# A product that adds a causal mask to the running maxima of an mLSTM scan, on fp32r operands instead of fp32 ones

## The chip, the cores and the metric

One Trainium2 chip, one core of it. The time is that of one execution on the device in microseconds (us), and lower is better. TensorE is called PE in the profile (PEld is its weight load), VectorE DVE, ScalarE ACT, GpSimd POOL, and SyncE SP.

## The reference

Two layers of a hybrid block over 256 context and 1024 latent tokens of width 1024. Each layer has a token mixer of four head groups and a feed-forward part: dense in the first layer, a mixture of eight experts in the second. The change lies in the mixer, where two recurrences run over the tokens in both directions. One is gated linear attention (GLA), the other the mLSTM, cut here to what the change touches:

```python
def mlstm_scan(q, k, v, ig, lf, state, with_output):
    ...
    cum = jnp.cumsum(lf, axis=3)
    ...
    mask = jnp.tril(jnp.ones((L, L), dtype=bool))
    d_log = jnp.where(mask, cum[..., :, None] - cum[..., None, :] + ig[..., None, :], -jnp.inf)
    inter_log = cum + m_prev[..., None]
    m_row = jnp.maximum(inter_log, jnp.max(d_log, axis=-1))
    s = jnp.exp(d_log - m_row[..., None]) * jnp.einsum('bhnld,bhnsd->bhnls', q, k)
    ...
```

The weight of source token s for target token l is an exponential, and it is zero where s lies behind l in the direction of the scan. The kernel gets that zero by adding 1e30 to the running maximum at the masked places before it takes the exponential of (value of s minus that maximum).

## The kernel before

The program is a row of phases with a barrier of all engines after each one, so nothing of a phase overlaps the next. In each of the two layers they are: a norm, the input projection, a Fourier mix, a spatial gate, the decays (`phase_decays`), the scan (`phase_scan`), the output gates, the output projection, and then the feed-forward part with its own norm. `phase_scan` (L809) is the one that the change touches. It runs once in each layer.

**The work of a scan.** The 1280 tokens stand in 10 tiles of 128. A unit is one tile in one direction, and a scan has 20 of them (`for u in range(U)`), the forward (`d = 0`) and the backward direction in turn. Each engine runs the same loop over the units with its own list of instructions, written out by hand. Semaphores tie the lists together. There is no scheduler.

**One unit on TensorE, in order.** All of it is fp32, and the profile records every fp32 product as two MATMUL and two LDWEIGHTS, the transposes as one each:

- L854, L856: transposes of a decayed key and of two key tiles.
- L861: identity times a 128x512 mask (`negF` or `negB`, 1e30 where masked and 0 elsewhere, four copies side by side, one for each head), written to the PSUM bank `MB` with `start=True`. For u of 1 and more it waits for `a_ex` of the unit before, that is for ScalarE's last read of that bank.
- L863: four products of depth 8, one for each head, that add the running maxima `mx`, broadcast over the 128 source rows, into the same bank. The last one raises `pe_mb`.
- L870: the mLSTM scores. It waits for `g_q`, GpSimd's masked copies of q, and for `v_w` of the unit before.
- L877: the GLA scores. It waits for `v_st` of the unit before, the new states of VectorE (in the first unit for `v_init`, VectorE's zeroing).
- L882, L884: products with the states `Sp` and `Sm`.
- L887: the GLA output. It waits for `v_sg`, VectorE's masked copy of the GLA scores (L950).
- L892: the mLSTM output. It waits for `v_w`, VectorE's product of weights and scores (L954).
- L897, L900: the updates of the states. The last one raises `pe_u`.

**The other engines.** ScalarE copies the transposed key out of PSUM (L911), then takes four exponentials of the bank `MB` into `ex` (L914). GpSimd makes the masked copies of q (L925, L927), two units ahead of TensorE's use of the buffers at most. VectorE has the longest list: `kw` (L947), L950, L954, the read of the GLA output (L958 or L960), then from L963 on the mLSTM output with its denominator (L963 to L977; where the tile has been written by the other direction, L974 and L975 take the place of L977), and then the updates of the states from L981 to L990. L990 writes `Sp` and raises `v_st`. Many of these steps wait for the one before them by a semaphore (`Chain`).

Of the kernel before, what the change touches and what calls it, by code (L numbers as in the profile page):

```python
# [15 lines left out]
F32R = mybir.dt.float32r  # L16
# [6 lines left out]
P = 128  # L23
# [9 lines left out]
NH, HD = 4, 64  # L33
# [775 lines left out]
def phase_scan(nc, io, S, l, FM, TM, M):  # L809

    U = 2 * NT
    with Phase(nc, f"scan{l}") as ph:
# [15 lines left out]
        g_q = ph.sem("masked_q_ready")  # L828
        qg = ph.sb("qg", [P, 2, NH, P])
        qm = ph.sb("qm", [P, 2, NH, P])  # L830
        v_init, v_kw, v_sg, v_w, v_og, v_om, v_st, ch = (ph.sem(n) for n in (
            "states_zero", "kw_ready", "gla_weights_ready", "mlstm_weights_ready", "gla_out_read", "mlstm_out_read", "states_ready", "dve_step"))
        ps, c = S["ps"], S["c"]
        mx, tg, dcol, qd, kd, em, vx, og, om = (M[k] for k in ("mx", "tg", "dcol", "qd", "kd", "em", "vx", "og", "om"))
        TR, SG, OG, KT, MB, SM, OI, OC = range(8)
# [3 lines left out]
        def unit(u):  # L839
            d = u % 2  # L840
            n = order(d, u // 2)
            return d, n, slice(n * P, (n + 1) * P)

        with nc.Block() as block:

            @block.tensor
            def _(pe):
                for u in range(U):
                    d, n, t = unit(u)

                    if u >= 1:
                        pe.wait_ge(a_kdt, u)
                        pe.wait_ge(v_kw, u)
                    nc.tensor.transpose(ps[:, KT, 0:P], kd[:, d, t], c("ident"))  # L854
                    for j in range(2):
                        x = nc.tensor.transpose(ps[:, TR, (j + 1) * P:(j + 2) * P], FM[:, mk[j], t], c("ident"))  # L856
                    x.then_inc(pe_tr, 1)

                    if u >= 1:
                        pe.wait_ge(a_ex, u)  # L860
                    nc.tensor.matmul(ps[:, MB, :], c("ident"), c("negF" if d == 0 else "negB"), start=True, stop=False, skip_group_check=True)  # L861
                    for h in range(NH):
                        x = nc.tensor.matmul(ps[:, MB, h * P:(h + 1) * P], sel8[0:8, 4 * d + h, :], mx[:, d, t],  # L863
                                             start=False, stop=(h == NH - 1), skip_group_check=True)
                    x.then_inc(pe_mb, 1)
                    if u >= 1:
                        pe.wait_ge(v_w, u)
                    pe.wait_ge(g_q, u + 1)
                    for j in range(2):
                        x = nc.tensor.matmul(ps[:, SM, j * 256:(j + 1) * 256], FM[:, mk[j], t],  # L870
                                             qm[:, d, 2 * j:2 * j + 2, :].rearrange("p a b -> p (a b)"), start=True, stop=True)
                    x.then_inc(pe_sm, 1)
                    if u >= 1:
                        pe.wait_ge(v_st, u)
                    else:
                        pe.wait_ge(v_init, 1)
                    nc.tensor.matmul(ps[:, SG, :], kd[:, d, t], qg[:, d, :, :].rearrange("p a b -> p (a b)"),  # L877
                                     start=True, stop=True).then_inc(pe_sg, 1)
                    if u >= 1:
                        pe.wait_ge(v_og, u)  # L880
                        pe.wait_ge(v_om, u)
                    nc.tensor.matmul(ps[:, OG, 0:256], qd[:, d, t], Sp[:, d, :], start=True, stop=False, skip_group_check=True)  # L882
                    for j in range(2):
                        nc.tensor.matmul(ps[:, OC, j * 130:(j + 1) * 130], FM[:, mq[j], t], Sm[:, d, j, :], start=True, stop=True)  # L884
                    pe.wait_ge(v_sg, u + 1)
                    for h in range(NH):
                        x = nc.tensor.matmul(ps[:, OG, h * HD:(h + 1) * HD], sg[:, d, h, :], TM[:, n, h * HD:(h + 1) * HD],  # L887
                                             start=False, stop=(h == NH - 1), skip_group_check=True)
                    x.then_inc(pe_og, 1)
                    pe.wait_ge(v_w, u + 1)  # L890
                    for h in range(NH):
                        x = nc.tensor.matmul(ps[:, OI, h * 65:(h + 1) * 65], ex[:, d, h, :], vx[:, n, h, :], start=True, stop=True)  # L892
                    x.then_inc(pe_om, 1)

                    pe.wait_ge(a_kdt, u + 1)
                    pe.wait_ge(v_og, u + 1)
                    nc.tensor.matmul(ps[:, OG, 256:512], kdt[:, d, :], TM[:, n, 0:256], start=True, stop=True)  # L897
                    pe.wait_ge(v_kw, u + 1)
                    for j in range(2):
                        x = nc.tensor.matmul(ps[:, SG, j * 130:(j + 1) * 130], kw[:, d, 2 * j:2 * j + 2, :].rearrange("p a b -> p (a b)"),  # L900
                                             vx[:, n, 2 * j:2 * j + 2, :].rearrange("p a b -> p (a b)"), start=True, stop=True)
                    x.then_inc(pe_u, 1)

            @block.scalar
            def _(act):
                for u in range(U):
                    d, n, t = unit(u)
                    if u >= 2:
                        act.wait_ge(pe_u, u - 1)
                    act.wait_ge(pe_tr, u + 1)  # L910
                    nc.scalar.copy(kdt[:, d, :], ps[:, KT, 0:P]).then_inc(a_kdt, 1)  # L911
                    act.wait_ge(pe_mb, u + 1)
                    for h in range(NH):
                        x = nc.scalar.activation(ex[:, d, h, :], ps[:, MB, h * P:(h + 1) * P], ACT.Exp,  # L914
                                                 bias=tg[:, n, d, 0, 4 * d + h:4 * d + h + 1], scale=-1.0)
                    x.then_inc(a_ex, 1)
# [1068 lines left out]
def build(nc, io):  # L1985
    S = {name: nc.dram_tensor(name, shape, F32, kind="Internal").ap() for name, shape in
         (("xT_d", (P, KD, T)), ("mixT_d", (P, KD, T)), ("xs_d", ((NUNIT + 1) * UNIT, D)), ("ys_d", (NUNIT * UNIT, D)), ("g2_d", (D,)), ("a_d", (P, DFF // P, T)))}
    with ExitStack() as top:
# [11 lines left out]
        for l in range(2):  # L2000
            ctx_out = l == 0
            groups = GROUPS if ctx_out else GROUPS[1:]
            with ExitStack() as lay:
                FM = sb(lay, f"FM{l}", [P, 9, T])
                TM = sb(lay, f"TM{l}", [P, NT, 1536])
                with ExitStack() as st:
                    hT = sb(st, f"hT{l}", [P, KD, T])

                    xT = TM[:, 0:7, :].rearrange("p a b -> p (a b)")[:, 0:KD * T].rearrange("p (k t) -> p k t", t=T)
                    phase_norm(nc, S, f"nm{l}", io["xT"] if l == 0 else S["xT_d"], xT, hT, l, 0, GROUPS)  # L2010
                    phase_project(nc, io, S, l, hT, FM, TM, ctx_out)
                phase_fourier(nc, io, S, l, FM, ctx_out)
                phase_sgu(nc, io, S, l, TM, ctx_out)
                M = {}
                M["qd"] = sb(lay, f"qd{l}", [P, 2, T])
                M["kd"] = sb(lay, f"kd{l}", [P, 2, T])
                M["em"] = sb(lay, f"em{l}", [P, 2, 3, NT])
                M["mx"] = sb(lay, f"mx{l}", [8, 2, T])
                M["ig"] = sb(lay, f"ig{l}", [8, T])
                M["tg"] = sb(lay, f"tg{l}", [P, NT, 2, 4, 8])  # L2020
                M["dcol"] = sb(lay, f"dcol{l}", [P, 4, NT])
                M["vx"] = sb(lay, f"vx{l}", [P, NT, NH, 65])
                phase_decays(nc, io, S, l, FM, TM, M)

                for name, ch in (("og", 0), ("om", 6)):
                    M[name] = FM[:, ch:ch + 2, :].rearrange("p a b -> p (a b)").rearrange("p (n c) -> p n c", c=256)
                phase_scan(nc, io, S, l, FM, TM, M)
                phase_mix_out(nc, io, S, l, TM, M, ctx_out)
# [67 lines left out]
```

## Time and profile before

| what | us |
|---|---|
| median of 3 runs | 6039.61 |
| lowest and highest of them | 6039.34 and 6043.22 |
| the profiled execution, its own time | 6042.35 |
| its span in the profile | 6040.4 |

The busy times of the whole span are 5266.8 us for TensorE, 2766.7 us for VectorE, 2003.3 us for ScalarE and 163.9 us for GpSimd. The two scans fill about 753 to 931 us and 2793 to 2971 us of it. The clock column (PEclk) gives the TensorE clock that was granted: 1.00 is 2.4 GHz, 0.50 is 1.2 GHz. The "idle before" of a row names what ended the idle time of that engine. The end of a matmul record is modelled, so records of products that follow each other overlap, and the time that a product takes from its engine is read from start to start.

### The profile page before, as it was taken

How to read it: one execution, taken by the hardware profiler on the slowest of the kernel's cores; microseconds unless marked ns; L12 is line 12 of the kernel's file. 1: busy time of each engine (PE TensorE's matmuls, PEld its weight loads, DVE VectorE, ACT ScalarE, POOL GpSimd, SP SyncE). 2: the span in 40 equal slices, each digit the busy share in tenths (PEclk: the TensorE clock that was granted, in tenths of full speed). 3: DMA queues.
4: the chain of work that ended last, by engine and by line, in shares of the span. 5: the costliest groups of instructions: out<-in, count | busy, mean ns of one | idle time of the engine just before them, and what ended most of it. 6: DMA issues, size and time to landing. Idle time of an engine off the chain costs nothing. (4 is left out here: it accounts for less than half of the span.)

```text
span 6040.4 us, 61280 instructions
## 1 busy us (share of the span) xinstructions
PE 5266.8 (87%) x22972; PEld 3985.7 (66%) x22973; DVE 2766.7 (46%) x2881; ACT 2003.3 (33%) x1995; POOL 163.9 (3%) x239
## 2 busy tenths in 40 slices
PE   6899395699997969975675999999999999999994
PEld 3444174488886755433555888888888888888883
DVE  0220474311113332116623844599659654448466
ACT  1100111211112230002112634477547544447453
POOL 0000020000000000001101000000000000000001
PEclk7899697799998989987885999999999999999996
DMA  9111003221115441010036955599759755558576
GB/s 382 28 43 52 18 1 133 80 65 56 57 46 169 135 148 31 22 65 1 23 139 262 346 186 197 206 381 380 256 207 382 293 183 204 196 182 340 200 274 226
DMA packets 262623, 996.66 MB, mean 165 GB/s; under 512 B 40000, under 2 KB 112384, under 8 KB 175744
## 3 DMA queue, kind: packets, MB, share of 16 engines
q1 hardware_dynamic: 243200, 926.43, 41.7%
q0 software_dynamic: 13040, 49.29, 2.2%
q10 hardware_dynamic: 6288, 19.66, 0.8%
q8 instruction: 61, 1.00, 0.1%
q14 instruction: 34, 0.28, 0.0%
HBM read 911.68 MB, written 83.63 MB: 165 GB/s over the span
## 5 line engine op out<-in xcount | busy, mean ns | idle before, releaser
L1697 PE MATMUL ps<-moe_gate_up_hi,moe_xh 128*128 128x512 f32 x2464 | 963.0, 391 | 9.3 <-DVE moe_gate_up_lo L1849 9.3
L1697 PE MATMUL ps<-moe_gate_up_hi,moe_xl 128*128 128x512 f32 x2464 | 960.7, 390 | 0.0
L1849 DVE TENSOR_TENSOR moe_gate_up_lo<-moe_wst,moe_gate_up_hi 128x2048 fp32r<-128x2048 f32 x424 | 952.2, 2284 | 17.7 <-ACT moe_gate_up_hi L1780 17.7
L1697 PE MATMUL ps<-moe_gate_up_lo,moe_xh 128*128 128x512 f32 x2464 | 959.6, 389 | 0.0
L1780 ACT CAST moe_gate_up_hi<-moe_wst 128x2048 fp32r<-128x2048 f32 x424 | 791.1, 1924 | 0.1
L1862 DVE TENSOR_TENSOR moe_down_lo<-moe_wst,moe_down_hi 128x2048 fp32r<-128x2048 f32 x210 | 480.1, 2289 | 159.1 <-ACT moe_down_hi L1794 158.6
L1697 PEld LDWEIGHTS ps<-moe_gate_up_hi,moe_xh 128*128 128x128 f32 x2464 | 463.2, 188 | 106.8 <-DVE moe_gate_up_lo L1849 11.6
L1697 PEld LDWEIGHTS ps<-moe_gate_up_hi,moe_xl 128*128 128x128 f32 x2464 | 463.2, 188 | 96.9
L1697 PEld LDWEIGHTS ps<-moe_gate_up_lo,moe_xh 128*128 128x128 f32 x2464 | 463.3, 188 | 95.5
L1868 DVE TENSOR_TENSOR moe_a<-moe_sil,ps 128x512 f32<-128x512 f32 x210 | 143.4, 683 | 739.2 <-ACT moe_sil L1800 739.2
L1800 ACT ACTIVATE moe_sil<-ps 128x512 f32<-128x512 f32 x210 | 125.9, 600 | 982.5 <-PE ps L1697 982.4
L1794 ACT CAST moe_down_hi<-moe_wst 128x2048 fp32r<-128x2048 f32 x210 | 404.2, 1925 | 72.6 <-PE ps L1717 72.6
L1256 PE MATMUL ps<-hh,up_wh 128*128 128x512 f32 (+1 forms) x1056 | 376.8, 357 | 51.2 <-DVE up_wl L1300 39.4
L1717 PE MATMUL ps<-moe_down_hi,moe_ah 128*128 128x512 f32 x1232 | 399.2, 405 | 9.7 <-DVE moe_al L1873 9.7
L403 PE MATMUL ps<-proj_w,hT 128*128 128x512 f32 x928 | 398.6, 592 | 0.0
L1717 PE MATMUL ps<-moe_down_lo,moe_ah 128*128 128x512 f32 x1232 | 383.0, 392 | 0.0
L1717 PE MATMUL ps<-moe_down_hi,moe_al 128*128 128x512 f32 x1232 | 380.4, 390 | 0.0
L1256 PE MATMUL ps<-hl,up_wh 128*128 128x512 f32 (+1 forms) x1056 | 374.4, 355 | 0.0
L1256 PE MATMUL ps<-hh,up_wl 128*128 128x512 f32 (+1 forms) x1056 | 374.2, 354 | 0.0
L400 PE MATMUL ps<-hT,proj_w 128*128 128x512 f32 (+1 forms) x832 | 307.9, 534 | 48.2 <-DMA proj_w<-in_w_in 48.2
L403 PEld LDWEIGHTS ps<-proj_w,hT 128*128 128x128 f32 x928 | 176.3, 190 | 221.9 <-issue 221.9
L400 PEld LDWEIGHTS ps<-hT,proj_w 128*128 128x128 f32 x832 | 161.3, 194 | 194.8 <-issue 136.8
(330 smaller groups left out, 6499.5 us busy)
## 6 DMA issues: line engine op xcount, KB each, us to landing
moe_wst<-in_moe_packed SPq DMA_DIRECT2D x634, 1024.0 KB, 6.7
ada_w<-in_ada_packed SPq DMA_DIRECT2D x24, 2048.0 KB, 26.4
down_wst<-in_ffn_w_down SPq DMA_DIRECT2D x66, 512.0 KB, 3.6
proj_w<-in_w_in SPq DMA_DIRECT2D x8, 2048.0 KB, 7.8
four_dft<-in_dft_seq SPq DMA_DIRECT2D x16, 1024.0 KB, 4.9
xs_d<-route_zero SPq DMA_DIRECT2D x1, 16384.0 KB, 50.8
moe_rows<-xs_d POOLq DMA_DIRECT2D x16, 1024.0 KB, 5.3
ys_d<-moe_y POOLq DMA_DIRECT2D x15, 1024.0 KB, 4.5
```

What stands on the lines that cost most here:

```text
L400: mm = nc.tensor.matmul(ps[:, u % NB, :n], wring[:, i % 2, k, j * P:(j + 1) * P], hT[:, k, a:a + n], start=(k == 0), stop=(k == KD - 1))
L403: mm = nc.tensor.matmul(ps[:, u % NB, :], hT[:, k, a * P:(a + 1) * P], wring[:, i % 2, k, :], start=(k == 0), stop=(k == KD - 1))
L1256: x = nc.tensor.matmul(ps[:, 2 * g + kind, :n], w[:, s, kind, k, :], h[:, k, t0:t0 + n], start=(k == 0 and j == 0), stop=(k == KD - 1 and ...
L1697: x = nc.tensor.matmul(ps[:, 2 * (q % 2) + i, :], xx[:, k, t], w[:, q % 2, k, :], start=(k == 0 and j == 0), stop=(k == KD - 1 and j == 2))
L1717: x = nc.tensor.matmul(ps[:, Y0 + 2 * i + half, :], aa[:, q % 2, i, c, :], w[:, q % 2, c, half * 512:(half + 1) * 512], start=(q == 0 and ...
L1780: nc.scalar.copy(guh[:, q % 2, 4 * j:4 * j + 4, :], wst[:, slot(n), :].rearrange("p (k n) -> p k n", k=4)).then_inc(hi, 1)
L1794: nc.scalar.copy(dnh[:, q % 2, :, :], wst[:, slot(n), :].rearrange("p (k n) -> p k n", k=2)).then_inc(hi, 1)
L1800: nc.scalar.activation(sil[:, :, :], ps[:, 2 * (q % 2):2 * (q % 2) + 2, 0:W], ACT.Silu).then_inc(silu, 1)
L1849: nc.vector.tensor_tensor(gul[:, q % 2, k, :], wst[:, slot(n), :].rearrange("p (k n) -> p k n", k=4), guh[:, q % 2, k, :].bitcast(F32), AL ...
L1862: nc.vector.tensor_tensor(dnl[:, q % 2, :, :], wst[:, slot(n), :].rearrange("p (k n) -> p k n", k=2), dnh[:, q % 2, :, :].bitcast(F32), AL ...
L1868: nc.vector.tensor_tensor(a[:, q % 2, :, :, :].rearrange("p i c f -> p i (c f)"), sil[:, :, :], ps[:, 2 * (q % 2):2 * (q % 2) + 2, W:2 * W ...
```

## The change

At the start of each scan ScalarE rounds three 128x128 tiles to fp32r, the format that TensorE takes in one pass: the identity and one copy of each mask. The mask product then reads these. Its moving operand is the one 128x128 mask, read four times with a step of zero between heads, and its output is the same 128x512 bank. In the first unit of a scan it waits for the rounding. All other products stay as they are.

```diff
@@ phase_scan
         qm = ph.sb("qm", [P, 2, NH, P])
+        unit_r = ph.sb("unit_r", [P, P], F32R)
+        neg_r = ph.sb("neg_r", [P, 2, P], F32R)
+        a_mask = ph.sem("masks_rounded")
...
                     if u >= 1:
                         pe.wait_ge(a_ex, u)
-                    nc.tensor.matmul(ps[:, MB, :], c("ident"), c("negF" if d == 0 else "negB"), start=True, stop=False, skip_group_check=True)
+                    if u == 0:
+                        pe.wait_ge(a_mask, 1)
+                    nc.tensor.matmul(ps[:, MB, :].rearrange("p (h t) -> p h t", t=P), unit_r[:, :],
+                                     neg_r[:, d, :].unsqueeze(1).to_broadcast([P, NH, P]), start=True, stop=False, skip_group_check=True)
...
             @block.scalar
             def _(act):
+                nc.scalar.copy(unit_r[:, :], c("ident"))
+                nc.scalar.copy(neg_r[:, 0, :], c("negF")[:, 0:P])
+                nc.scalar.copy(neg_r[:, 1, :], c("negB")[:, 0:P]).then_inc(a_mask, 1)
                 for u in range(U):
```

ScalarE's list around the start of the first scan, before and then after (dec is the phase of the decays, scan that of the scan):

```order
63 L723 ACTIVATE dec_dec<-dec_dec 8x20
64 L655 UNCONDITIONAL_BRANCH
65 L904 UNCONDITIONAL_BRANCH
66 L911 COPY scan_kdt<-ps 128x128
67 L914 ACTIVATE scan_ex<-ps,tg 128x128 x4
```

```order
63 L723 ACTIVATE dec_dec<-dec_dec 8x20
64 L655 UNCONDITIONAL_BRANCH
65 L910 UNCONDITIONAL_BRANCH
66 L912 CAST scan_unit_r<-cst 128x128
67 L913 CAST scan_neg_r<-cst 128x128
68 L914 CAST scan_neg_r<-cst 128x128
69 L920 COPY scan_kdt<-ps 128x128
70 L923 ACTIVATE scan_ex<-ps,tg 128x128 x4
```

Three casts stand ahead of ScalarE's first copy. No other instruction came in. On TensorE the first unit, with its waits, reads so before and after:

```order
269 L854 MATMUL ps<-cst,kd 128x128
270 L856 MATMUL ps<-cst,FM 128x128 x2
271 L861 MATMUL ps<-cst 128x512
272 L863 MATMUL ps<-mx,cst 128x128 x4
273 L870 MATMUL ps<-scan_qm,FM 128x256 [waits scan0_masked_q_ready]
```

```order
269 L857 MATMUL ps<-cst,kd 128x128
270 L859 MATMUL ps<-cst,FM 128x128 x2
271 L866 MATMUL ps<-scan_neg_r,scan_unit_r 128x512 [waits scan0_masks_rounded]
272 L869 MATMUL ps<-mx,cst 128x128 x4
273 L876 MATMUL ps<-scan_qm,FM 128x256 [waits scan0_masked_q_ready]
```

The mask product keeps its place in the order, changes its operands, and in the first unit has a wait that it did not have. In the later units its wait is the same as before. The lists of VectorE and GpSimd are unchanged but for line numbers.

## Rows read from the trace of the kernel before

**Rows 1.** The page, costs by engine: busy us, share of the span, instructions.
```profile
PE 5266.8 (87%) x22972; PEld 3985.7 (66%) x22973; DVE 2766.7 (46%) x2881; ACT 2003.3 (33%) x1995; POOL 163.9 (3%) x239
```

**Rows 2.** Groups by line and shape, 753 to 930 us (first scan): busy, mean ns.
```profile
L861 PE MATMUL ps<-cst 128*128 128x512 f32 x40 | 21.4, 617 | 0.0
```

**Rows 3.** Waits, 762 to 925 us: who for whom, us, times, longest.
```profile
PEld ps L877 <- DVE scan_Sp L990: 13.6, 19, 1.0
```

**Rows 4.** Timeline of one unit of the first scan: start, us, engine, line.
```profile
764.17 0.43 DVE L963 TENSOR_TENSOR scan_tmp<-ps,tg 128x260 f32<-128x260 f32 x1 [0.47 <-PE ps L892]
...
765.23 1.02 PE L861 MATMUL ps<-cst 128*128 128x512 f32 x2
...
766.19 1.15 PE L863 MATMUL ps<-mx,cst 8*128 8x128 f32 x8
...
767.27 1.13 PE L870 MATMUL ps<-scan_qm,FM 128*128 128x256 f32 x4
...
768.10 0.35 DVE L990 TENSOR_SCALAR scan_Sp<-scan_Sg,em 128x256 f32<-128x256 f32 x1
...
768.49 0.30 PEld L877 LDWEIGHTS ps<-scan_qg,kd 128*128 128x128 f32 x2 [0.50 <-DVE scan_Sp L990]
...
769.66 0.73 DVE L950 COPY_PREDICATED scan_sg<-cst,ps 128x512 f32<-128x512 int32 x1 [0.76 <-PE ps L877]
...
770.45 1.10 PE L887 MATMUL ps<-TM,scan_sg 128*128 128x64 f32 x8
...
772.49 0.43 DVE L963 TENSOR_TENSOR scan_tmp<-ps,tg 128x260 f32<-128x260 f32 x1 [0.47 <-PE ps L892]
```

**Rows 5.** The same, weight load of a unit whose tile was written before.
```profile
785.58 0.30 PEld L877 LDWEIGHTS ps<-scan_qg,kd 128*128 128x128 f32 x2 [0.96 <-DVE scan_Sp L990]
```

**Rows 6.** Timeline of the output projection, TensorE, fp32r products, low and full clock.
```profile
1018.65 0.63 PE L1104 MATMUL ps<-op_mix,op_w_parts 128*128 128x512 f32 x1
...
1019.93 0.63 PE L1104 MATMUL ps<-op_mix,op_w_parts 128*128 128x512 f32 x1
...
1022.28 0.39 PE L1104 MATMUL ps<-op_mix,op_w_parts 128*128 128x512 f32 x1
...
1022.96 0.39 PE L1104 MATMUL ps<-op_mix,op_w_parts 128*128 128x512 f32 x1
```

**Rows 7.** Timeline of the first unit of the first scan.
```profile
753.03 0.18 PEld L854 LDWEIGHTS ps<-cst,kd 128*128 128x128 f32 x1 [1.92 <-issue]
...
753.52 0.55 PEld L861 LDWEIGHTS ps<-cst 128*128 128x128 f32 x2
...
754.14 1.17 POOL L927 TENSOR_TENSOR scan_qm<-FM,cst 128x256 f32<-128x256 f32 x2
...
755.36 0.49 DVE L937 MEMSET scan_Sm<- 128x520 f32 x1
755.57 1.78 PEld L863 LDWEIGHTS ps<-mx,cst 8*128 8x128 f32 x8 [1.50 <-issue]
...
759.44 1.87 PE L877 MATMUL ps<-scan_qg,kd 128*128 128x512 f32 x2
...
762.14 1.10 PE L887 MATMUL ps<-TM,scan_sg 128*128 128x64 f32 x8
```

**Rows 8.** Groups by line and shape, ScalarE: busy us, mean ns.
```profile
L911 ACT COPY scan_kdt<-ps 128x128 f32<-128x128 f32 x40 | 10.6, 266 | 227.3 <-PE ps L856 227.3
L1385 ACT CAST down_ah<-down_ast 128x256 fp32r<-128x256 f32 x22 | 8.8, 400 | 0.0
```

**Rows 9.** Windows: length, busy us (instructions) of PE, PEld, DVE, ACT, POOL, granted clock, DMA share, GB/s.
```profile
757.40:761.80 4.40, 4.40 (x12) 2.79 (x11) 0.45 (x1) 1.14 (x4) 0.39 (x2) 0.58 0.00 0
804.00:925.00 121.00, 116.45 (x671) 87.54 (x670) 90.55 (x233) 19.73 (x70) 28.33 (x39) 1.00 0.00 1
929.00:931.00 2.00, 0.00 (x0) 0.00 (x0) 1.89 (x6) 0.00 (x0) 0.00 (x0) 1.00 0.00 0
1868.00:1892.00 24.00, 19.60 (x156) 18.70 (x156) 10.92 (x14) 9.05 (x15) 0.00 (x0) 1.00 0.58 184
```

## The prediction

> **What bounds the kernel now.** I first read the busy times of the page. They make TensorE look like the bound, at 87% of the span [rows 1]. That share is mostly the projections and the experts, and it says nothing of the scan, so I then read the scan alone. Its window at full clock has TensorE busy for 116.45 of 121 us [rows 9]. A reader would stop here and call every TensorE instruction in it expensive. But a record's end is modelled and records overlap, so "busy" hides small waits. The view that decides is the list of waits, and then the timeline of one unit.
>
> The list of waits has the weight load of L877 waiting 19 times for VectorE's L990, 13.6 us in all, 0.72 us each [rows 3]. That is once for every unit but the first. The timeline shows what this means [rows 4]. In one unit VectorE starts L963 at 764.17 and ends L990 at 768.10 + 0.35 = 768.45. The weight load of L877 starts at 768.49, 0.04 us later. TensorE has its own work meanwhile: L861 from 765.23, L863 from 766.19, L870 from 767.27 to 768.40. So VectorE's piece ends last and releases L877. Then come L877, L950 at 769.66, L887 at 770.45, L892, and L963 again at 772.49. One turn, from L963 to L963, takes 772.49 - 764.17 = 8.32 us, and L861, L863 and L870 are not on it: they lie in TensorE's side branch between the updates of one unit and L877 of the next. In a unit whose tile was written before, VectorE has one more instruction, and the weight load waits 0.96 us instead of 0.50 us [rows 5].
>
> The first unit of each scan is different. No state is pending there, the clock is at its low level, 1.2 GHz, and TensorE works through its list without a real wait until L877 at 759.44, while VectorE's zeroing ended at 755.36 + 0.49 = 755.85 [rows 7]. There L861 is on the path. The clock reaches 2.4 GHz late in the window from 757.40 to 761.80, whose mean is 0.58 [rows 9]. (0.58 - 0.50) x 2 x 4.40 = 0.7 us of it were at the full level, so it rose at about 761.1.
>
> **The warm units (19 of 20 in each scan, 38 in all).** The mask product has 40 records in the first scan, two a unit, of 617 ns on average [rows 2]. They overlap, so the price is read from start to start: it holds TensorE from 765.23 to 766.19, 0.96 us [rows 4]. The nearest price for the new one is the fp32r product of the same shape in the output projection. Three of them pass between two rows of one operand pair, 0.68 us at full clock (1022.28 to 1022.96), or 0.23 us each [rows 6]. So each unit takes 0.96 - 0.23 = 0.73 us off TensorE's branch. The zero step in the moving operand has no row here. I take it at the price of an ordinary operand. At worst it costs as much as before, and since it sits in the branch that is off the path the sum is the same.
>
> Off the path means: L863 and L870 start 0.73 us earlier, L877 still waits for L990, and its weight load now waits about 0.50 + 0.73 = 1.2 us. ScalarE's exponentials (L914) move up by 0.73 us. Nobody waited for them, since VectorE reads `ex` in L954, after L950, which waits for L877. GpSimd is released by L877, which does not move. The warm units therefore give 0 us. The two ends for them: a gain of at most 38 x 0.05 = 1.9 us, if L870's end at 768.40 had some hold on the start of L877 at 768.49, and a loss of nothing from the work itself. I take 0, since L877 follows L990 by the same 0.04 us here.
>
> **The first unit (twice).** Before: the first weight load of L861 starts at 753.52 and that of L863 at 755.57, 2.05 us [rows 7]. After: L861 has to wait for three casts. No row shows a 128x128 cast to fp32r. The 128x256 one takes 400 ns and the 128x128 copy out of PSUM 266 ns [rows 8]. These two are my bounds, and I take 0.29 us, near the copy because the width is the same. The casts start with the phase, at about 753.1 (TensorE's first weight load is at 753.03 [rows 7]), and end at 753.1 + 3 x 0.29 = 754.0. The weights then take 0.27 us (0.55 us for two loads of L861 [rows 7]), and the product itself, at low clock, 1.28 us for three, so 0.43 us [rows 6]. L863 can load at 754.0 + 0.27 + 0.43 = 754.7 instead of 755.57, a gain of 0.9 us, which would be 0.6 us with casts of 0.40 us. ScalarE's own first copy, L911, waits for the transposes until about 754.0 anyway and is not held up. L870 then stands at about 756.6, after GpSimd's copies of that unit (754.14 + 1.17 = 755.31) and after the zeroing (755.85) [rows 7], so the gain reaches L877.
>
> Part of it is given back, because the clock rises by the clock on the wall and not with my work. If it still rises at 761.1, L877 starts 0.9 us earlier, at 758.5, and so does L882, and both run at 1.2 GHz to the end, as does some of L884. L884 and what follows then do at the low level about 0.9 us of work that took 0.45 us at the high one. L887, at 762.14 before [rows 7], comes 0.5 us earlier. The second scan has the same order and the same start, so it gives 0.5 us too.
>
> **Sum.** 38 x 0 - 2 x 0.5 = -1.0 us. Against the profiled execution that is 6042.35 - 1.0 = 6041.4, and against the median, which lies 2.7 us lower, 6039.6 - 1.0 = 6038.6. The phases end in barriers, so what the scans gain passes to the end. The memory of the two new tiles is the scan's own and moves nothing else.
>
> **Rival A, slower: the clock drops inside the scan.** The change lets TensorE stand idle for 1.2 or 1.7 us in every unit. If that brings the clock to 1.2 GHz in the scan, L877 to L900 take twice as long, and these are on the path. A warm unit has about 8.3 - 0.5 - 0.73 = 7.1 us of TensorE work, and cold it takes 14.2 us, which TensorE then bounds: 14.2 - 8.3 = 5.9 us more for each cold unit. Three cold units of 38 make the kernel slower by more than can be told from nothing, and half of them cost 19 x 5.9 = 112 us, 6151 us. Against it: the clock stayed at its full level from 1868 to 1892 us, with TensorE busy for only 19.60 of 24 us, 82% [rows 9]. The changed scan has about 7.1 of 8.3, or 86%. After the last product of the scan TensorE was idle through the whole window from 929 to 931, and the clock was still 1.00 [rows 9]. The gaps that I expect are shorter than that. The Trainium skill, page TensorE: Matmul & The Clock Gate, section "A second HAM failure mode: psum-queue depth-cycling", says that short idles between groups of matmuls, frequent enough, make the clock swing between its levels. By that rule this rival is what happens. The trace does not agree so far, since such idles of 0.5 to 1 us once a unit left the clock at 1.00 for 121 us. I give it 4%.
>
> **Rival B, faster: TensorE's list is the bound after all.** If the waits of 0.5 us in front of L877 are a lead of the weight load over a product that could not have started sooner, each warm unit gets shorter by up to 0.73 us: 38 x 0.73 + 1 = 29 us, 6011 us. For it: L870's end at 768.40 and L877's start at 768.50 nearly touch. Against it: VectorE would have to end its piece earlier too, and L963 to L990 are a closed piece that depends on L892 and L900, not on L861. I give it 3%. The Trainium skill, page TensorE: Matmul & The Clock Gate, section "Back-to-back issue gap", has about 131 ns for a product of 512 columns in a stream of loads and products. The trace says 230 ns [rows 6], so the measurement decides. By the page this rival would gain 0.83 us a unit, 32 us.
>
> **Rival C: the product does not get shorter**, because the repeated operand or the accumulation of fp32 products on top of it costs a full four passes. Nothing in the trace speaks for it, and the total would be 6039.6 plus up to 0.5 us for the wait on the casts in each scan, 6040.6. I give it 3%.
>
> **How the numbers follow.** A measurement of this kernel can tell 0.2%, about 12 us, from no change. My case has 88%, rival A 4%, B 3%, C 3%, and 2% are for a change of the runs that has nothing to do with it. My case and C lie within 12 us. Predicted time 6038.6 us. For the range: the gain can be 1.9 us + 2 x 0.9 = 3.7 us, and the runs of before spread by 3.9 us, which gives 6039.6 - 3.7 - 3.9 = 6032. Upward: no gain, one rise of the clock that comes later in one scan, so that the outputs and updates of the first unit (L887 to L900, about 2.7 us) run at the low level and cost as much again, and the same spread, 6039.6 + 2.7 + 3.9 = 6046. Chances: faster 0.03, same 0.92, slower 0.05.
>
> **What would show it.** Right: one MATMUL of the mask line per unit, 40 in all, of 0.39 us. The weight load of L877's successor waits 1.2 us for VectorE in the shorter units and 1.7 us in the others. A turn of 8.3 or 8.8 us as before. L877 of the first unit at 0.9 us less behind the start of the phase, the next one at 0.5 us less. Clock 1.00 from the second unit on. Wrong: a clock under 1.00 in the middle of a scan (A), a turn under 8.0 us (B), or two records of the mask line per unit (C).

## The result: 0.28% slower

| kernel | median us | lowest to highest | runs |
|---|---|---|---|
| before | 6043.22 | 6039.34 to 6045.48 | 7 |
| changed | 6059.68 | 6054.85 to 6064.69 | 7 |

The ratio is 1.0028, with a 95% interval from 1.0017 to 1.0040, about 17 us. The forecast was 6038.6 us with a range up to 6046, and no difference that can be told. It was wrong, and the time came out on the other side. The profiled execution of the changed kernel took 6060.06 us, its span is 6058.4 us.

In the changed kernel L866 is the mask product, L869 the running maxima, L876 the mLSTM scores, L883 the GLA scores, L888 and L890 the products with the states, L893 and L898 the outputs, L959 VectorE's masked copy, L972 its first step on the mLSTM output, and L999 its write of `Sp`. The page's row of the engines answers to [rows 1]:

```profile
PE 5262.2 (87%) x22932; PEld 3999.0 (66%) x22933; DVE 2767.2 (46%) x2881; ACT 2003.6 (33%) x2001; POOL 163.6 (3%) x239
```

TensorE has 40 records fewer, one for each of the 40 units. Its busy time fell by only 4.6 us, though the records of the mask product fill 9.9 us of each scan instead of 21.4, which is 23 us less in all. Something else got longer. TensorE's weight loads got 13.3 us longer, and no other engine changed by more than 1 us. The windows of the two scans, with the columns of [rows 9], say what it was:

```profile
804.00:925.00 121.00, 109.28 (x610) 86.94 (x610) 84.18 (x219) 18.96 (x68) 28.35 (x39) 0.92 0.00 1
...
2804.00:2966.00 162.00, 144.87 (x815) 114.14 (x816) 112.07 (x287) 25.99 (x93) 43.58 (x60) 0.92 0.00 1
```

The window of the first scan had clock 1.00 and 671 TensorE instructions before [rows 9]. Now it has clock 0.92 and 610, and the records that the mask product no longer has, one a turn, are only some 14 of the 61 that are missing. The waits from 755 to 942 us, in the form of [rows 3], show the idle time that the change makes:

```profile
PEld ps L883 <- DVE scan_Sp L999: 25.5, 19, 1.6
...
PE ps L883 <- DVE scan_Sp L999: 17.9, 19, 1.2
```

The weight load of the GLA scores waited 13.6 us in 19 units before and waits 25.5 us now. The timeline of the first turns, in the form of [rows 4], shows both at work:

```profile
766.74 0.47 PE L866 MATMUL ps<-scan_neg_r,scan_unit_r 128*128 128x512 f32 x1
...
767.14 1.15 PE L869 MATMUL ps<-mx,cst 8*128 8x128 f32 x8
...
768.22 1.13 PE L876 MATMUL ps<-scan_qm,FM 128*128 128x256 f32 x4
...
769.68 0.35 DVE L999 TENSOR_SCALAR scan_Sp<-scan_Sg,em 128x256 f32<-128x256 f32 x1
...
770.08 1.89 PE L883 MATMUL ps<-scan_qg,kd 128*128 128x512 f32 x2 [0.73 <-DVE scan_Sp L999]
...
771.76 1.06 PE L888 MATMUL ps<-scan_Sp,qd 128*128 128x256 f32 x2
...
772.61 1.07 PE L890 MATMUL ps<-scan_Sm,FM 128*128 128x130 f32 x4
...
773.48 1.13 PE L893 MATMUL ps<-TM,scan_sg 128*128 128x64 f32 x8
...
779.86 1.13 PE L883 MATMUL ps<-scan_qg,kd 128*128 128x512 f32 x2 [0.73 <-DVE scan_Sp L999]
```

The branch before L883 runs as forecast. L876 ends at 769.35 and L883 waits 0.73 us for VectorE. But L883 then takes 1.89 us where it took 1.12 us in a warm turn before, and L888 takes 1.06 us where it took 0.59 us. The granted clock of three windows around it:

```profile
770.00:771.00 1.00, 0.92 (x2) 0.41 (x3) 0.45 (x2) 0.00 (x0) 0.00 (x0) 0.66 0.00 0
772.00:773.20 1.20, 1.20 (x5) 1.02 (x5) 1.20 (x2) 0.00 (x0) 1.08 (x2) 0.50 0.00 0
773.20:774.40 1.20, 1.20 (x11) 1.20 (x10) 0.10 (x1) 0.00 (x0) 1.09 (x2) 0.78 0.00 0
```

Just after the wait the clock falls from 2.4 to 1.2 GHz, and some 3.4 us later it is back. From L883 to L883 this turn takes 779.86 - 770.08 = 9.78 us. A turn of that kind takes 8.32 us [rows 4], so one fall costs 1.46 us. In windows of 1 us from the second unit to the last product there are 9 falls in the first scan and 6 in the second, 15 in all. Before there was none. From the first weight load to the end of the last L999 the scans took 177.9 and 178.4 us before and 190.4 and 186.6 us now, 20.6 us more. Fifteen falls are 21.9 us, and the first units gave 1.4 us back (below). That is 20.5 us, so nothing in the scans is left over to explain. The spans of the two profiled executions differ by 18.0 us, so the other phases, which the change does not touch, took 2.6 us less.

Theory: in each turn TensorE stands idle 0.6 us longer, and these idle times let the clock fall on TensorE's part of the path. Rivals: the fp32r format, or the kind of work, brings the falls, and not the idle time.

### The profile page after: what moved, and what is told of

The parts are those of the page before. It is cut to its first block and busy times, and to the rows that moved or that the text cites. A ratio compares the mean times of both kernels' runs of the same rounds, so it can differ in the third digit from the quotient of the medians.

```text
span 6058.4 us, 61208 instructions
## 1 busy us (share of the span) xinstructions
PE 5262.2 (87%) x22932; PEld 3999.0 (66%) x22933; DVE 2767.2 (46%) x2881; ACT 2003.6 (33%) x2001; POOL 163.6 (3%) x239
```

## Experiments

All times are medians beside the kernel before on the same chip, whose median was 6041.61 to 6042.75 us on the chips of the experiments. Falls were counted in the one profiled execution of each kernel, in windows of 1 us, from the second unit to the last product of each scan. "Idle" is the wait of TensorE's products in front of the GLA scores, in shorter and in longer turns, at full clock.

| kernel | idle, us | falls | median us | ratio to before, 95% interval |
|---|---|---|---|---|
| before | about 0.1 / 0.55 | 0 | | 1 |
| changed | 0.72 / 1.19 | 15 | 6059.68 | 1.0028 (1.0017 to 1.0040) |
| product twice | 0.49 / 0.95 | 12 | 6058.59 | 1.0029 (1.0017 to 1.0040) |
| product three times | 0.26 / 0.72 | 13 | 6056.52 | 1.0022 (1.0012 to 1.0032) |
| product four times | 0.02 / 0.49 | 0 | 6042.08 | 1.0000 (0.9991 to 1.0010) |
| product five times | 0 / 0.26 | 0 | 6042.18 | 1.0001 (0.9991 to 1.0011) |
| fp32r forward only | 0.72 / 1.18, every second turn | 1 | 6042.92 | 1.0001 (0.9991 to 1.0011) |
| fp32r in three of four units | 0.72 / 1.19, three of four | 10 | 6052.53 | 1.0018 (1.0008 to 1.0027) |
| fp32, a small VectorE instruction | 0.29 / 0.75 | 7 | 6061.55 | 1.0031 (1.0019 to 1.0044) |
| fp32, two VectorE instructions | 1.01 / 1.47 | 17 | 6102.27 | 1.0097 (1.0080 to 1.0114) |
| fp32, the two in forward units | 1.02 / 1.48, every second turn | 8 | 6071.19 | 1.0051 (1.0034 to 1.0068) |

The eleven profiled executions of this table have 418 waits in front of the GLA scores, 38 in each. Of the 224 that lasted at most 0.56 us none was followed by a fall. Of the 194 that lasted 0.71 us or more 83 were, and these are all the falls there are.

### The same fp32r product, issued two to five times

```diff
-                    nc.tensor.matmul(ps[:, MB, :]..., unit_r[:, :],
+                    for _ in range(3):
+                        nc.tensor.matmul(ps[:, MB, :]..., unit_r[:, :],
```

Each repetition overwrites the one before it, so nothing changes but TensorE's time. Three times:

> The changed kernel with its fp32r mask product issued three times in a row instead of once, so that TensorE is about as busy as with the fp32 one (0.40 us for the first and 0.23 us for each further one, 0.86 us against 0.96 us). Theory of the idle time: the falls of the clock inside the scans (15 in the changed kernel) come from TensorE standing idle longer before L883, so they go away here and the time is that of the kernel before, 6042 us, with the first units' gain within 1 us. Rival, the fp32r format itself brings the falls: they stay, about 6060 us.

Twice:

> The fp32r mask product issued twice. Theory of the idle time: the wait before L883 is about 0.5 us in the shorter turns and 0.95 us in the longer ones, between the two kernels; some falls stay, fewer than 15, and the time lies between 6042 and 6060 us, nearer to 6042. Rival, the format: as many falls as with one product, 6060 us.

Neither came out so: 6056.52 us with 13 falls (the expectations below have 12, without the one in the very last unit) and 6058.59 us with 12. The theory looked beaten, until the timeline with three products was read:

```profile
783.55 0.94 PE L867 MATMUL ps<-scan_neg_r,scan_unit_r 128*128 128x512 f32 x3
784.42 1.15 PE L870 MATMUL ps<-mx,cst 8*128 8x128 f32 x8
785.50 1.13 PE L877 MATMUL ps<-scan_qm,FM 128*128 128x256 f32 x4
787.35 1.12 PE L884 MATMUL ps<-scan_qg,kd 128*128 128x512 f32 x2 [0.72 <-DVE scan_Sp L1000]
```

Three take 784.42 - 783.55 = 0.87 us, and the idle time of a longer turn is 0.72 us, still 0.17 us more than the 0.55 us of before. The step from no falls to 13 could lie in that. So I issued it four and five times.

> The fp32r mask product issued four times, 1.10 us in all against 0.96 us for the fp32 one, so that TensorE's idle time before L883 is shorter than in the kernel before (0 to 0.4 us). Theory of the idle time: with no more idle time than before, no falls of the clock inside the scans, and 6042 us (at most 3 us more, since L876 now ends 0.1 us after VectorE in the shorter turns). Rival, the format: the falls stay as with three products (12, 6057 us).

> The fp32r mask product issued five times, 1.33 us in all. TensorE now ends its branch about 0.3 us after VectorE in the shorter turns and has about 0.2 us of idle time in the longer ones. Theory of the idle time: no falls, about 20 shorter turns at 0.3 us more, 6048 us. Rival, the format: falls and that cost, 6060 us or more.

```profile
785.49 1.13 PE L884 MATMUL ps<-scan_qg,kd 128*128 128x512 f32 x2 [0.49 <-DVE scan_Sp L1000]
```

```profile
804.00:925.00 121.00, 117.37 (x699) 92.83 (x698) 90.45 (x233) 19.73 (x70) 28.21 (x39) 1.00 0.00 1
```

The first fence is a longer turn with four products, the second the same window as above for that kernel. Its idle time is 0.49 us, the clock is 1.00, and the time is 6042.08 us, the time of the kernel before. With five it is 6042.18 us, not the 6048 us that I had allowed for TensorE ending last. Its shorter turns still take 8.32 us. TensorE's work in such a turn is just that long: the 7.95 us found below for the fp32 product, less its 0.96 us, plus 1.33 us. The format is innocent: the kernel with four times as much fp32r work has no falls. More work for TensorE makes this kernel 14 to 17 us faster, a step of 14 us from three products to four.

### The idle time alone, all in fp32

```diff
+                    step(nc.vector.tensor_tensor(spare[:, 0:4], dsg[:, 0:4], dsg[:, 4:8], ALU.add))
                     nn = order(d, min(u // 2 + 1, NT - 1))
                     nc.vector.tensor_scalar(Sp[:, d, :], ...).then_inc(v_st, 1)
```

> The kernel before, all fp32, with one small VectorE instruction (128x4, about 0.2 us with its semaphore) ahead of L990 in every unit. Its own cost is 40 x 0.2 = 8 us, 6050 us. TensorE's idle time before L877 becomes 0.3 and 0.75 us, which is what three fp32r products gave. Theory of the idle time: about a dozen falls, 12 x 1.46 = 18 us more, 6068 us. Rival, the format or the kind of work: no falls, 6050 us.

It took 6061.55 us, 19 us more than before for an instruction of 0.15 us in each of 40 units. Two turns of its timeline:

```profile
876.09 1.98 PE L878 MATMUL ps<-scan_qg,kd 128*128 128x512 f32 x2 [0.75 <-DVE scan_Sp L992]
...
895.49 1.12 PE L878 MATMUL ps<-scan_qg,kd 128*128 128x512 f32 x2 [0.75 <-DVE scan_Sp L992]
```

```profile
804.00:925.00 121.00, 114.15 (x630) 84.63 (x629) 88.62 (x239) 19.73 (x70) 28.36 (x39) 0.97 0.00 1
```

The falls are there without any fp32r. The two rows also show what no count of idle time explains: the same wait of 0.75 us is followed by a fall in one turn (1.98 us for L878) and by none in another (1.12 us). The profile has 7 falls, not the dozen that I expected, and the scans of the profiled execution are 17.9 us longer, which is 8 us for the instruction and 7 x 1.46 = 10 us for the falls. Two larger instructions, of 0.45 us each, in the same place:

> The kernel before, all fp32, with two more VectorE instructions (128x256, about 0.45 us each) ahead of L990 in every unit, which adds 36 us by itself, 6078 us, and makes TensorE idle 1.0 and 1.45 us before L877. Theory of the idle time: at least the 15 falls of the changed kernel, 22 us more, 6100 us. Rival, the format or the kind of work: clock 1.00 through the warm part of both scans, 6078 us.

6102.27 us and 17 falls: 60 us more, where 36 us for the instructions and 17 x 1.46 = 25 us for the falls make 61. Two of these falls are unlike the others: the clock stayed at 1.2 GHz for about 10 us, into the next turn (from 798.1 to 808.3 and from 941.5 to 951.7 us).

### Every second turn, three of four turns

> Only the forward direction's units read the fp32r operands, the backward ones keep the fp32 product, so every second turn has the longer idle time. Theory of the idle time: falls only where the mean idle share is high enough, fewer than 15, 6042 to 6052 us. Rival, the format: about half of the falls, 6051 us, all of them in or right after forward units.

```diff
-                    nc.tensor.matmul(ps[:, MB, :]..., unit_r[:, :], neg_r[:, d, :]...)
+                    if d == 0:
+                        nc.tensor.matmul(ps[:, MB, :]..., unit_r[:, :], neg_r[:, d, :]...)
+                    else:
+                        nc.tensor.matmul(ps[:, MB, :], c("ident"), c("negB"), start=True, stop=False, skip_group_check=True)
```

```profile
902.44 1.13 PE L886 MATMUL ps<-scan_qg,kd 128*128 128x512 f32 x2 [0.55 <-DVE scan_Sp L1002]
911.21 1.13 PE L886 MATMUL ps<-scan_qg,kd 128*128 128x512 f32 x2 [1.18 <-DVE scan_Sp L1002]
```

```profile
804.00:925.00 121.00, 111.90 (x660) 86.52 (x659) 90.39 (x234) 19.67 (x70) 26.17 (x36) 1.00 0.00 1
```

6042.92 us, one fall. Here TensorE's busy records fill 111.90 of 121 us and the clock stays up, while with three fp32r products everywhere they filled more, and the clock fell:

```profile
804.00:925.00 121.00, 114.61 (x650) 90.37 (x650) 85.31 (x220) 18.62 (x67) 28.39 (x39) 0.94 0.00 1
```

Records get longer at the low clock, so a window with falls in it looks busier than it is. The window that ends before the first fall of that scan avoids this, first with three products everywhere, then with fp32r in the forward units only:

```profile
804.00:885.00 81.00, 77.48 (x465) 61.30 (x465) 59.77 (x154) 12.97 (x47) 21.84 (x30) 1.00 0.00 1
```

```profile
804.00:885.00 81.00, 75.52 (x445) 58.22 (x444) 61.02 (x160) 14.05 (x50) 19.63 (x27) 1.00 0.00 1
```

The busier of the two is the one in which the falls then came. In the longer turns too TensorE idles less in it, 0.72 us in each against 0.56 and 1.18 us in turn, 0.87 us on average. So the busy share of a scan doesn't decide it. That suggested that several turns with a long idle time must follow each other, and I tested this from both sides.

> As the changed kernel, but every fourth unit keeps the fp32 mask product, so three turns with the longer idle time (0.7 or 1.2 us) are followed by one with 0.1 or 0.55 us. If each turn by itself can bring a fall, three quarters of the 15 falls stay, 11 of them, about 6055 us. If a row of such turns is needed, as the one fall in the run with every second turn suggests, clearly fewer, 6042 to 6050 us.

> The kernel before, all fp32, with the two more VectorE instructions (0.9 us) in the forward units alone: after each of these TensorE idles 1.0 or 1.45 us, after the backward ones 0.1 or 0.55 us. The instructions cost 20 x 0.9 = 18 us, 6060 us. If the length of a single idle time decides, at least 8 falls (half of the 17 of the run with all units), 6072 us or more. If it takes a row of turns, few or no falls, 6060 us.

Three of four turns gave 10 falls and 6052.53 us, about in proportion. Every second turn with idle times of 1.02 and 1.48 us gave 8 falls and 6071.19 us, where 6060 had been expected if a row of turns were needed, and at least 8 falls and 6072 if not. Two of them, each between turns with short idle times:

```profile
878.86 2.08 PE L878 MATMUL ps<-scan_qg,kd 128*128 128x512 f32 x2 [1.47 <-DVE scan_Sp L993]
888.98 1.12 PE L878 MATMUL ps<-scan_qg,kd 128*128 128x512 f32 x2 [0.56 <-DVE scan_Sp L993]
898.68 1.68 PE L878 MATMUL ps<-scan_qg,kd 128*128 128x512 f32 x2 [1.48 <-DVE scan_Sp L993]
```

A fall needs no row of long turns. That part of the idea is refuted, and the other side's eight falls came. But the length of the wait alone does not give the number of falls either. Three products had 13 falls in 18 waits of 0.72 us, all in the longer turns. The changed kernel had 4 falls in its 20 waits of 0.72 us, in the shorter turns, and 11 in its 18 of 1.19 us. The forward-only kernel had 1 in 18 waits of 0.72 and 1.18 us. Why it had so few stays open.

### Using the time that the change frees

L877 (L883 in the changed kernel) waits for the new states but doesn't read them. It must only not overwrite the bank of the updates before L983 has read it. The wait for the states belongs to L882, which does read `Sp`.

```diff
                     if u >= 1:
-                        pe.wait_ge(v_st, u)
-                    else:
-                        pe.wait_ge(v_init, 1)
+                        pe.wait_ge(v_rd, u)
                     nc.tensor.matmul(ps[:, SG, :], ...).then_inc(pe_sg, 1)
                     if u >= 1:
                         pe.wait_ge(v_og, u)
                         pe.wait_ge(v_om, u)
+                        pe.wait_ge(v_st, u)
+                    else:
+                        pe.wait_ge(v_init, 1)
...
-                                            c("blockm").unsqueeze(1).to_broadcast([P, 2, 130]), ALU.mult)
+                                            c("blockm").unsqueeze(1).to_broadcast([P, 2, 130]), ALU.mult).then_inc(v_rd, 1)
```

With the fp32 mask product:

> The kernel before, all fp32, but L877 no longer waits for the new states, which it doesn't read. It waits for L983, VectorE's last read of the bank that L877 writes, and the wait for L990 moves to L882. TensorE then has 8.2 us of work a turn without a wait and becomes the bound: 0.1 us less in the shorter turns, 0.57 us less in the longer ones, some 12 us over both scans, 6030 us, and the clock stays at 1.00 since TensorE hardly idles. If the states were not what it waited for: 6042 us.

6018.29 us, ratio 0.9963 (0.9949 to 0.9977), no falls. In its timeline L875 is the GLA scores and L883 the product with `Sp`:

```profile
840.32 0.35 DVE L991 TENSOR_SCALAR scan_Sp<-scan_Sg,em 128x256 f32<-128x256 f32 x1
...
840.46 1.02 PE L875 MATMUL ps<-scan_qg,kd 128*128 128x512 f32 x2
...
841.32 0.59 PE L883 MATMUL ps<-scan_Sp,qd 128*128 128x256 f32 x2
...
849.27 0.59 PE L883 MATMUL ps<-scan_Sp,qd 128*128 128x256 f32 x2
```

L875 starts before L991 has ended, and TensorE has no wait left. A turn is 849.27 - 841.32 = 7.95 us. I had put TensorE's work at 8.2 us a turn, which is why 6030 was too high. I had taken the modelled end of L870's record (1.13 us) for the end of its work. Here L875 starts 0.97 us after it, and L883 starts 0.86 us after L875, where the kernel before needed 0.96 us behind its wait. So TensorE had about 0.26 us to spare in a shorter turn before, not 0.1 us. With the fp32r product:

> The same edit on the changed kernel. The mask product is now on the path, and TensorE has 7.6 us of work a turn. Theory of the idle time: TensorE idles under 0.5 us a turn, so the clock stays at 1.00, the turns take 7.6 to 8.0 us, and the two scans give 28 us, 6014 us. Rival: the clock still falls some 15 times, 22 us given back, 6036 us.

6007.33 us, ratio 0.9941 (0.9925 to 0.9958), no falls. L881 is the GLA scores here, L1000 the write of `Sp`:

```profile
844.88 1.02 PE L881 MATMUL ps<-scan_qg,kd 128*128 128x512 f32 x2
...
845.36 0.35 DVE L1000 TENSOR_SCALAR scan_Sp<-scan_Sg,em 128x256 f32<-128x256 f32 x1
...
845.86 0.67 PE L889 MATMUL ps<-scan_Sp,qd 128*128 128x256 f32 x2
```

```profile
804.00:900.00 96.00, 93.92 (x577) 75.89 (x576) 78.91 (x208) 18.27 (x65) 26.17 (x36) 1.00 0.00 1
```

TensorE is not quite without waits here: in 7 turns up to 900 us L889 waits up to 0.42 us for L1000. That is less than the 0.55 us of the kernel before.

The same mask product that cost 17 us now gains 11 us over its fp32 twin (the scans are 322.5 us together instead of 334.3 us). With VectorE's L950 ahead of L947 on top:

> As the one before, and VectorE does L950, on which L887 waits, ahead of L947. The longer turns lose up to 0.3 us more if TensorE was waiting for L950 there: 6009 us, clock at 1.00. If TensorE is the bound in all turns already, the same as the one before.

6002.42 us, ratio 0.9932 (0.9916 to 0.9949), no falls, and scans of 319.1 us together, 3.5 us less. It is the fastest version here, about 41 us below the kernel before by its ratio.

## Why the prediction was wrong

**What held.** VectorE's L963 to L990 is the piece that releases the GLA scores, and the mask product lies on TensorE's side branch. The weight load's wait grew from 0.50 to 1.13 us in the shorter turns and from 0.96 to 1.59 us in the longer ones. Turns without a fall kept their 8.3 and 8.8 us. Casts held up nothing but the first unit. Had the clock stayed up, the forecast would have held within the noise: with four products, the same wait for the casts and no falls, the time is that of the kernel before.

**The step that failed** is the term of the warm units, 38 x 0 us, with "a loss of nothing from the work itself". It measured 21.9 us: 15 falls of the clock in the 38 warm turns, each on TensorE's part of the path and each 1.46 us. The prediction knew this mechanism as rival A and weighed it at 4%. It was the right mechanism with the right place. Its size was off too: I priced half of the 38 warm turns as cold throughout, at 5.9 us, 6151 us, while the clock comes back after some 3.4 us. The Trainium skill, page TensorE: Matmul & The Clock Gate, section "A second HAM failure mode: psum-queue depth-cycling", describes a kernel in which frequent short idles between groups of matmuls make the clock swing, and by that rule this rival is what happens. The runs agree with it: 15 falls with idle times of 0.72 and 1.19 us, none with 0.49 us at most.

Behind the 4% stands a misread row. The prediction took the wait of the weight load, 0.50 and 0.96 us, for TensorE's idle time, and said that idles of 0.5 to 1 us had left the clock at 1.00 for 121 us. But the product itself waits less than its weight load. Before, L870 ends at 768.40 and L877 starts at 768.50 [rows 4], 0.10 us, and in a longer turn it is 0.55 us:

```profile
785.58 1.13 PE L877 MATMUL ps<-scan_qg,kd 128*128 128x512 f32 x2 [0.55 <-DVE scan_Sp L990]
```

So the change raised the idle time from 0.10 and 0.55 us to 0.72 and 1.19 us, beyond everything that those 121 us had shown. They say that 0.55 us is harmless, not that 0.72 us is. The kernel before stood close to the step: an instruction of 0.15 us brings the falls.

Two more pieces of evidence made me discount the rival, and neither bore on it.

- The window from 1868 to 1892 us, with TensorE 82% busy at clock 1.00 [rows 9], is another kind of work. The runs above show that the busy share does not order even the scans among themselves.
- The idle window from 929 to 931 at clock 1.00 [rows 9] shows one idle time once, and it ends too early: the clock is at 0.80 in the window from 931.5 to 932.0 us and at 0.50 in the one behind it. A fall follows some of the same waits and not others, so one case without a fall says little against 38 tries.

**Terms that were off a little.** The first unit gained 1.06 us, not 0.9. The casts follow each other by 0.20 us, not 0.29 us, since their records overlap, and the timeline of the first unit shows it:

```profile
755.35 0.18 PEld L857 LDWEIGHTS ps<-cst,kd 128*128 128x128 f32 x1 [1.93 <-issue]
755.36 0.30 ACT L912 CAST scan_unit_r<-cst 128x128 fp32r<-128x128 f32 x1 [7.18 <-PEq L135]
...
755.56 0.29 ACT L913 CAST scan_neg_r<-cst 128x128 fp32r<-128x128 f32 x1
...
755.76 0.29 ACT L914 CAST scan_neg_r<-cst 128x128 fp32r<-128x128 f32 x1
756.11 0.29 PEld L866 LDWEIGHTS ps<-scan_neg_r,scan_unit_r 128*128 128x128 f32 x1 [0.25 <-ACT scan_neg_r L914]
...
756.83 1.78 PEld L869 LDWEIGHTS ps<-mx,cst 8*128 8x128 f32 x8 [0.44 <-issue]
...
760.70 1.92 PE L883 MATMUL ps<-scan_qg,kd 128*128 128x512 f32 x2
```

L883 comes 760.70 - 755.35 = 5.35 us after the first weight load, against 759.44 - 753.03 = 6.41 us [rows 7]. At the second turn's GLA scores 0.74 us of it is left in the first scan and 0.62 us in the second (I had 0.5), 1.4 us in all. That this came out near is partly luck, since it hangs on the moment at which the clock rises: from the first GLA scores to the second it took 9.06 and 9.51 us in the two scans before, and 9.38 and 9.95 us now. The product holds TensorE for 0.40 us (766.74 to 767.14), not 0.23. Each further one of the same kind adds 0.23 us, so the other 0.17 us come once. No run here shows from what. Rival B was wrong for the reason given: TensorE's branch did end earlier, and the turn didn't move. Rival C was wrong too: 0.40 us is less than half of the 0.96 us of before.

## What to carry to other kernels

Work taken off an engine's side branch is not free of risk on TensorE: it becomes idle time, and where that idle time recurs every turn, as here every 8 to 9 us, the clock can fall on the products that are on the path. Before removing such work, read how much TensorE waits per turn now and after, and treat the largest wait that recurred without a fall (0.56 us here) as the only one that is known to be safe. The gain comes when the freed time is moved onto the path, here by letting a product wait for what it really needs: 17 us lost became 34 us won.

## What was not expected of the hardware

- A step between close values: with 0.55 us as the longest idle time there were no falls, with 0.72 us 13 (fp32r) and with 0.75 us 7 (fp32). Adding 0.23 us of idle-filling work took 14 us off the kernel.
- A fall follows the idle time, not the whole turn: all 83 falls begin in the wait or at most 0.55 us after it, and the full clock is back some 3.4 us later, but for the two stretches of about 10 us with two more VectorE instructions in every unit. In the changed kernel the falls near the end of each scan come once a turn, about 10.2 us apart.
- Which of equal waits is followed by a fall is not settled. Whether the moment at which the wait comes matters, and not only its length, was not tested. Runs of one kernel differ in it: with three products the times lie between 6050.18 and 6061.46 us, and with three of four units in fp32r between 6043.22 and 6058.67 us, where the kernel before lay between 6037.94 and 6045.43 us and between 6037.24 and 6046.01 us.
